# A reversed bias table by 128 one-row transfers on GpSimd's queue, one modulation unit as a block, and key copies on VectorE

## The chip, the cores and the metric

The kernel runs on one core of one Trainium2 chip. The metric is the device time of one execution in microseconds; the kernel before takes 2218.84 us (median of three runs, 2218.35 to 2221.72). It holds two transformer blocks of two layers each, in one program. Each engine (TensorE, VectorE, ScalarE, GpSimd, and SyncE for transfers) runs its own list of instructions in the order in which they are written, and semaphores join the lists.

## The reference

Sequence length 256, width 1024, batch 1, all in float32. The change lies in the two layers of the first block. A layer projects the normed input by one wide matrix into the inputs of three attention branches and their gates:

```
mod = c_act @ w_ada[l] + b_ada[l]
shift, scale, gate = [m[:, None, :] for m in split_cols(mod, (D, D, D))]
h = rms_norm(x, g_pre[l]) * (1.0 + scale) + shift
(cq, ckv, kr, za, qb_, kb_, vb_, zb, qc, kc, vc, zc, gcols) = split_cols(h @ w_in[l], IN_SPLITS)
...
kv = (rms_norm(c_kv, g_kv) @ w_ukv).reshape(B, S, MLA_HEADS, MLA_NOPE + MLA_V)
k_pe = rope(k_r, cos[None], sin[None])
k = jnp.concatenate([kv[..., :MLA_NOPE],
                     jnp.broadcast_to(k_pe[:, :, None, :], (B, S, MLA_HEADS, MLA_ROPE))], axis=-1)
```

Branch a has 8 heads and no bias. Branches b (8 heads, a window of 128, a sink) and c (4 differential heads) add a bias to the scores that depends only on the distance of key and query, `rel_bias[t5_bucket(kpos - qpos)]`, for 12 heads in all. The second block (a recurrent and a forgetting attention mixer, a gated linear attention, a dense and a mixture-of-experts feed-forward) is not touched.

## The kernel before

Activations lie transposed, 128 features by 256 tokens a tile. Weights stream from HBM through `ring`, six slots of 1 MB, filled by SyncE's queue in a fixed order (`stream`). Item n goes into slot n mod 6, and its transfer waits until item n-6 is released (`freed_at`). As the queue is in order, one item that waits holds all behind it.

A projection (`project`) of 128 output columns is 24 matmuls of 128x256: each weight is split into an upper part (`form_upper`, ScalarE, L1465) and a rest (`lower`, VectorE, L2107), and the three products of parts run on lines L697 to L699. ScalarE forms the upper part four projections ahead. The results take four PSUM banks in turn (`claim`): a bank is used again when the instruction that empties it has reported.

**The modulation.** The rows of `w_ada` are weighted and summed on VectorE, a unit (l, i) of two ring items in eight steps (`modulation_step`, L2021 and L2023), after which both slots are released. TensorE then sums over partitions (`modulation`, L887). Unit (0, 4) occupies items 16 and 17. Its eight steps stand two by two between the `lower` calls for the projection `zb`. Item 22, the second half of unit (0, 5), goes into the slot of item 16, and item 23, the weights of `qc`, into the slot of item 17. Item 21 goes into the slot of item 15 (`ukv`), which is released when the projection of the values `va` (L945) is done. Item 27 (`kc`) goes into a slot of unit (0, 5).

**The bias table.** A line of 512 biases per head is computed once (`bias_lines`) and written to HBM (`scratch`, L1605). One transfer on ScalarE's queue (L1614) reads it back into `table_up` with partition p shifted by p, so that the order of the partitions is the wrong way round. TensorE turns it with `flip`, a reversed identity: 12 matmuls of 128x384 (L952), each copied to `table` by ScalarE (L1645). VectorE reads `table` when it adds the bias to the scores of the first head of branch b (L2122).

**The keys of branch a.** The matmuls `kn` give two heads a bank; ScalarE copies each half to its place (`two_heads`), and later copies the rotated rows to all heads (`krows`, L1637 and L1638).

After `ukv` TensorE's order is kn 0 to 3, va 0 and 1, the 12 table matmuls (layer 0 only), kb, vbt, zb 0 to 3, the sum of unit (0, 4), qc 0 to 3, the sum of unit (0, 5), kc 0 to 3, and so on, and then the units of attention (`run_units`), 8 for a branch.

Of the kernel before, what the change touches and what calls it, by code (L numbers as in the profile page):

```python
# [43 lines left out]
def shape_constants(S):  # L44
# [27 lines left out]
    for c in range(4):  # L72
# [3 lines left out]
    flip = np.eye(P)[::-1]  # L76
# [3 lines left out]
               flip=flip, iota=iota)  # L80
# [20 lines left out]
def two_blocks(nc, A, C, out, known):  # L101
# [26 lines left out]
    def sem(name):  # L128
        return ctx.enter_context(nc.semaphore(name))
# [76 lines left out]
    table_up, lines = split(flat[:, 0:12 * 384], 12, 384), flat[:, 4608:5120]  # L206
# [19 lines left out]
    flip = vc[:, 1, 0:P]  # L226
# [123 lines left out]
    ada_ready, modsum_ready, table_ready = sem("ada_ready"), sem("modsum_ready"), sem("table_ready")  # L350
    proj_ready, kb_cleared = sem("proj_ready"), sem("kb_cleared")
    kc_moved, kc_halves = sem("kc_moved"), sem("kc_halves")
# [259 lines left out]
    def _(pe):  # L612
# [190 lines left out]
        def scores(u):  # L803
            br, l, i, _ = u
            b = claim("attn", ("s", br, l, i), *((exp_ready, "exp", br, l, i) if br == "a" else (scored, br, l, i)))
            if br == "a":
                pe.wait_ge(rope_ready, when(rope_ready, "q", l, i))
                pe.wait_ge(proj_ready, when(proj_ready, "krows", l))
# [82 lines left out]
        for l in range(L):  # L891
# [48 lines left out]
            for m_ in range(4):  # L940
                chunk(("kn", l, m_), "gemm", proj_ready, ("kn", l, m_), 1,
                      lambda k: w[:, 0, P * m_:P * m_ + P], lambda k: cq[:, 2])
# [5 lines left out]
            if l == 0:  # L948
                pe.wait_ge(table_in, when(table_in, "all"))
                for i in range(12):  # L950
                    b = claim("gemm", ("table", i), table_ready, "table", i)
                    nc.tensor.matmul(b[:, 0:384], flip, table_up[:, i], start=True, stop=True)\  # L952
                        .then_inc(psum_ready, wrote("table", i))
# [453 lines left out]
    def _(act):  # L1407
# [145 lines left out]
        for l in range(L):  # L1553
# [10 lines left out]
            if l == 0:  # L1564
# [13 lines left out]
                fetch(loaded_tables, flip, C["flip"])  # L1578
# [32 lines left out]
            if l == 0:  # L1611
                act.wait_ge(lines_out, when(lines_out, "all"))
                shifted = bass.AP(tensor=scratch.tensor, offset=0, ap=[[1, P], [512, 12], [1, 384]])
                act.dma_start(table_up, shifted).then_inc(table_in, tick(table_in, "all", by=16))  # L1614
# [16 lines left out]
            for c in range(4):  # L1631
                two_heads("kn", c, k_full)
            for t in range(NT):
                copy_out(("va", l, t), va[:, t], n=512)
            act.wait_ge(rope_ready, when(rope_ready, "k", l))
            every = krope[HEAD:HEAD + ROPE].unsqueeze(1).broadcast_to([ROPE, 4, S])
            nc.scalar.activation(kn[HEAD:HEAD + ROPE], every, ACT.Copy)  # L1637
            nc.scalar.activation(gates[HEAD:HEAD + ROPE, 20:24], every, ACT.Copy)\  # L1638
                .then_inc(proj_ready, tick(proj_ready, "krows", l))
            for n in range(2):  # L1640
                form_behind(("qb1", l), n)
            if l == 0:
# [1292 lines left out]
```

## Time and profile before

| | |
|---|---|
| median of three runs | 2218.84 us (2218.35 to 2221.72) |
| profiled execution | 2218.4 us, of which its span is 2216.6 us |
| TensorE busy (matmul) | 2137.2 us, 96% |
| VectorE busy | 1621.7 us, 73% |
| ScalarE busy | 1292.6 us, 58% |
| GpSimd busy | 26.7 us, 1% |
| granted TensorE clock | 0.979 of full speed, mean |

Matmuls are pipelined and their ends are modelled, so the busy time of TensorE says only that it has work. The places where it has none are read from the timeline and from the chain of waits.

### The profile page before, as it was taken

What the parts mean: (1) busy time and instruction counts of PE and PEld (TensorE: products, weight loads), DVE (VectorE), ACT (ScalarE), POOL (GpSimd) and SP (SyncE); (2) the same over time, 40 slices, a digit from 0 to 9 for tenths busy, and PEclk for the clock granted to TensorE, in tenths of its full rate; (3) what the DMA queues carried; (4) which work ended last, traced back from release to release, by engine and by line L of the source; (5) the groups of instructions that cost most, each with busy time, mean ns of one, the idle gap of its engine ahead of it and who ended that gap; (6) DMA issues with size and microseconds to landing.
All of it is one profiled execution on the core that took longest, in us unless ns stands there. A gap on an engine that the chain in (4) does not pass through costs nothing.

```text
span 2216.6 us, 33306 instructions
## 1 busy us (share of the span) xinstructions
PE 2137.2 (96%) x12812; PEld 1900.1 (86%) x12812; DVE 1621.7 (73%) x1938; ACT 1292.6 (58%) x1560; POOL 26.7 (1%) x19
## 2 busy tenths in 40 slices
PE   6899999999999999999998999999999999999997
PEld 5799999899999989998996888878888888888886
DVE  6557865558855765555636889888888889889896
ACT  2535533555523754433625777777777777777775
POOL 0000000000000300000000000000000000000000
PEclk7999999999999999998999999999999999999999
DMA  9776455556335424553546999989999999999990
GB/s 292 186 225 193 149 156 133 121 189 190 115 115 161 160 84 145 191 172 116 193 147 243 359 349 352 375 319 372 329 360 349 360 335 358 367 331 364 330 365 29
DMA packets 361195, 536.39 MB, mean 242 GB/s; under 512 B 67724, under 2 KB 207936, under 8 KB 361096
## 3 DMA queue, kind: packets, MB, share of 16 engines
q1 hardware_dynamic: 355536, 530.81, 70.1%
q10 hardware_dynamic: 5560, 4.19, 0.6%
q8 instruction: 70, 1.15, 0.2%
q14 instruction: 29, 0.24, 0.0%
HBM read 533.89 MB, written 1.07 MB: 241 GB/s over the span
## 4 chain that ended last, share of the span: by engine, by line
PE 88%; DVE 5%; ACT 3%; issue 2%; DMA 1%; ACTq 0%; DVEq 0%; SPq 0%
PE bank L697 24%; PE bank L699 23%; PE bank L698 23%; PE bank L644 5%; PE bank L849 2%; PE bank L1304 1%; ACT w_hi L1951 1%; PE bank L1252 1%; PE bank L657 1%; PE bank L1351 1%; DVE w_lo L2753 1%; PE bank L832 1%; DVE piece_lo L2385 1%; PE bank L818 1%; PE bank L822 1%
## 5 line engine op out<-in xcount | busy, mean ns | idle before, releaser
L2753 DVE TENSOR_TENSOR w_lo<-pool,w_hi 128x2048 fp32r<-128x2048 f32 x336 | 764.1, 2291 | 110.5 <-ACT w_hi L1951 110.0
L1951 ACT ACTIVATE w_hi<-pool 128x2048 fp32r<-128x2048 f32 x336 | 643.2, 1917 | 140.8 <-PE bank L699 140.8
L697 PE MATMUL bank<-w_hi,xe_hi 128*128 128x512 f32 x896 | 357.9, 399 | 12.7 <-DVE w_lo L2753 8.9
L699 PE MATMUL bank<-w_hi,xe_lo 128*128 128x512 f32 x896 | 350.2, 391 | 0.0
L698 PE MATMUL bank<-w_lo,xe_hi 128*128 128x512 f32 x896 | 349.8, 390 | 0.0
L697 PE MATMUL bank<-h_upper,upper 128*128 128x256 f32 x992 | 295.4, 298 | 3.4 <-DVE h_lo L2197 3.2
L698 PE MATMUL bank<-h_lo,upper 128*128 128x256 f32 x992 | 283.1, 285 | 0.0
L699 PE MATMUL bank<-h_upper,ring_lo 128*128 128x256 f32 x992 | 282.9, 285 | 0.0
L2107 DVE TENSOR_TENSOR ring_lo<-ring,upper 128x1024 fp32r<-128x1024 f32 x132 | 160.4, 1221 | 114.0 <-ACT upper L1465 113.7
L2385 DVE TENSOR_TENSOR piece_lo<-ring,piece_hi 128x1024 fp32r<-128x1024 f32 x118 | 144.9, 1236 | 109.3 <-ACT piece_hi L1454 109.1
L697 PEld LDWEIGHTS bank<-w_hi,xe_hi 128*128 128x128 f32 x896 | 168.6, 188 | 57.2 <-DVE w_lo L2753 17.2
L699 PEld LDWEIGHTS bank<-w_hi,xe_lo 128*128 128x128 f32 x896 | 168.4, 188 | 36.5
L697 PEld LDWEIGHTS bank<-h_upper,upper 128*128 128x128 f32 x992 | 192.6, 194 | 6.5 <-issue 4.5
L698 PEld LDWEIGHTS bank<-w_lo,xe_hi 128*128 128x128 f32 x896 | 168.9, 188 | 33.0
L697 PE MATMUL bank<-left_hi,piece_hi 128*128 128x256 f32 x672 | 193.0, 287 | 2.4 <-DVE left_lo L2407 2.4
L698 PEld LDWEIGHTS bank<-h_lo,upper 128*128 128x128 f32 x992 | 192.7, 194 | 2.0 <-issue 0.5
L699 PEld LDWEIGHTS bank<-h_upper,ring_lo 128*128 128x128 f32 x992 | 192.4, 194 | 0.0
L698 PE MATMUL bank<-left_lo,piece_hi 128*128 128x256 f32 x672 | 190.7, 284 | 0.0
L699 PE MATMUL bank<-left_hi,piece_lo 128*128 128x256 f32 x672 | 190.7, 284 | 0.0
L697 PE MATMUL bank<-w_hi,hT_hi 128*128 128x512 f32 x448 | 175.9, 393 | 0.0
L699 PE MATMUL bank<-w_hi,hT_lo 128*128 128x512 f32 x448 | 174.5, 389 | 0.0
L698 PE MATMUL bank<-w_lo,hT_hi 128*128 128x512 f32 x448 | 174.4, 389 | 0.0
(403 smaller groups left out, 3445.8 us busy)
## 6 DMA issues: line engine op xcount, KB each, us to landing
pool<-in_od_exp_w SPq DMA_DIRECT2D x336, 1024.0 KB, 6.8
ring<-in_w_in SPq DMA_DIRECT2D x48, 1024.0 KB, 5.4
ring<-in_ev_ffn_w SPq DMA_DIRECT2D x33, 1024.0 KB, 5.1
ring<-in_w_ada SPq DMA_DIRECT2D x24, 1024.0 KB, 8.3
ring<-in_od_w_in SPq DMA_DIRECT2D x12, 1024.0 KB, 5.2
ring<-in_ev_w_in SPq DMA_DIRECT2D x10, 1024.0 KB, 5.4
ring<-in_w_in SPq DMA_DIRECT2D x32, 256.0 KB, 4.5
ring<-in_w_out SPq DMA_DIRECT2D x8, 1024.0 KB, 4.8
```

Source lines behind the costliest of these rows:

```text
L644: m = nc.tensor.matmul(b[base:base + rows, 0:cols], left(k), right(k), start=(k == 0), stop=(k == K - 1))
L657: m = nc.tensor.matmul(b[:, at + t:at + t + 1], tile[:, k, P * t:P * t + P], mean[scale][:, 0:1], start=start and t == 0, stop=stop, skip_ ...
L697: nc.tensor.matmul(b, left[0], right[0], start=first, stop=False, skip_group_check=True)
L698: nc.tensor.matmul(b, left[0], right[1], start=False, stop=False, skip_group_check=True)
L699: return nc.tensor.matmul(b, left[1], right[0], start=False, stop=last, skip_group_check=True)
L818: m = nc.tensor.matmul(s, q_full(i)[0:HEAD + ROPE, tok], k_full(i)[0:HEAD + ROPE], start=True, stop=True)
L822: m = nc.tensor.matmul(s, qc[:, i // 2, tok], (kc, kc_odd)[i % 2][:, i // 2], start=True, stop=True)
L849: m = nc.tensor.matmul(b[:, 0:S], v[:, k, at:at + P], pT[:, k], start=(k == 0), stop=(k == NT - 1))
L1951: nc.scalar.activation(w_hi[q % 3], ring_slot(q), ACT.Copy)\
L2107: V.tensor_tensor(dst, src, split(upper[:, n % PIECES], KD, P).bitcast(F32), ALU.subtract)\
L2385: V.tensor_tensor(lo, src, hi.bitcast(F32), ALU.subtract).then_inc(piece_ready, tick(piece_ready, n))
L2753: V.tensor_tensor(w_lo[q % 3], ring_slot(q), w_hi[q % 3].bitcast(F32), ALU.subtract).then_inc(item_vector, tick(item_vector, "lo", q))
```

## The change

The part of the table that turns it on TensorE, with `flip`, `table_up` and the 12 copies on ScalarE, goes. GpSimd issues 128 transfers, one for a partition, which put the shifted line of partition 127-p straight into row p of `table`. VectorE waits for all of them where it first reads the table. Unit (0, 4) becomes one block ahead of the rotation of the keys. The eight key copies of a layer go from ScalarE to VectorE, behind the rotation of the queries, and `krows` goes behind the values of branch c.

```
-            if l == 0:
-                pe.wait_ge(table_in, when(table_in, "all"))
-                for i in range(12):
-                    b = claim("gemm", ("table", i), table_ready, "table", i)
-                    nc.tensor.matmul(b[:, 0:384], flip, table_up[:, i], start=True, stop=True)\
-                        .then_inc(psum_ready, wrote("table", i))
...
-                fetch(loaded_tables, flip, C["flip"])
...
             if l == 0:
                 act.wait_ge(lines_out, when(lines_out, "all"))
-                shifted = bass.AP(tensor=scratch.tensor, offset=0, ap=[[1, P], [512, 12], [1, 384]])
-                act.dma_start(table_up, shifted).then_inc(table_in, tick(table_in, "all", by=16))
...
-            for c in range(4):
-                two_heads("kn", c, k_full)
...
-            if l == 0:
-                for i in range(12):
-                    b = psum(act, "table", i)
-                    nc.scalar.activation(table[:, i], b[:, 0:384], ACT.Copy)\
-                        .then_inc(table_ready, tick(table_ready, "table", i))
...
+            act.wait_ge(rope_ready, when(rope_ready, "k", l))
+            every = krope[HEAD:HEAD + ROPE].unsqueeze(1).broadcast_to([ROPE, 4, S])
+            nc.scalar.activation(kn[HEAD:HEAD + ROPE], every, ACT.Copy)
+            nc.scalar.activation(gates[HEAD:HEAD + ROPE, 20:24], every, ACT.Copy)\
+                .then_inc(proj_ready, tick(proj_ready, "krows", l))
...
             if br != "a":
+                if l == 0:
+                    dve.wait_ge(table_in, when(table_in, "all"))
...
+            if l == 0:
+                modulation(0, 4)
...
+            for c in range(4):
+                b = psum(dve, "kn", l, c)
+                V.tensor_copy(k_full(2 * c)[0:HEAD], b[0:HEAD, 0:S])
+                V.tensor_copy(k_full(2 * c + 1)[0:HEAD], b[HEAD:P, 0:S]).then_inc(kn_ready, tick(kn_ready, l, c))
...
             for c in range(4):
-                two_steps(0, 4, c)
                 lower((("zb" + "1" * (c // 2), l), c % 2))
...
+        pool_engine.wait_ge(lines_out, when(lines_out, "all"))
+        for p in range(P):
+            row = bass.AP(tensor=scratch.tensor, offset=P - 1 - p, ap=[[12 * 512, 1], [512, 12], [1, 384]])
+            pool_engine.dma_start(table[p:p + 1], row).then_inc(table_in, tick(table_in, "all", by=16))
```

On TensorE, this is the place behind the keys and values of branch a (L945 or L944 is va, the rows from L697 or L695 are kb). Before:

```order
L644 MATMUL bank<-pool,ring 128x256 [waits rope_ready] x2
L945 MATMUL bank<-ring,pool 128x512 [waits proj_ready] x2
L952 MATMUL bank<-pool 128x384 [waits proj_ready,table_in]
L952 MATMUL bank<-pool 128x384 [waits proj_ready] x3
L952 MATMUL bank<-pool 128x384 [waits table_ready] x8
L697 MATMUL bank<-h_upper,upper 128x256 [waits lower_ready,table_ready]
L698 MATMUL bank<-h_lo,upper 128x256
```

And now:

```order
L642 MATMUL bank<-pool,ring 128x256 [waits rope_ready] x2
L944 MATMUL bank<-ring,pool 128x512 [waits kn_ready] x2
L695 MATMUL bank<-h_upper,upper 128x256 [waits lower_ready,kn_ready]
L696 MATMUL bank<-h_lo,upper 128x256
L697 MATMUL bank<-h_upper,ring_lo 128x256
```

The 12 matmuls are gone, kb follows va at once, and va waits for the key copies on VectorE.

On VectorE, this is the place where the normed latents are finished (L2269 or L2254) and the rotation of the keys begins (L2275 or L2262). Before:

```order
L2072 RECIPROCAL rstd<-rstd 128x256 [waits root_ready]
L2269 SCALAR_TENSOR_TENSOR pool<-pool,vecs,rstd 128x256 [waits rstd_ready]
L2275 TENSOR_TENSOR tmp<-bank,pool 128x256 [waits psum_ready]
L2276 TENSOR_TENSOR pool<-pool 128x256
L2277 TENSOR_TENSOR pool<-pool,tmp 128x256 [waits dve_step]
```

And now:

```order
L2055 RECIPROCAL rstd<-rstd 128x256 [waits root_ready]
L2254 SCALAR_TENSOR_TENSOR pool<-pool,vecs,rstd 128x256 [waits rstd_ready]
L2004 TENSOR_SCALAR probsT<-ring,small 128x512 [waits slot_loaded5,slot_loaded4,psum_ready]
L2006 SCALAR_TENSOR_TENSOR probsT<-ring,small,probsT 128x512 [waits ada_step] x7
L2262 TENSOR_TENSOR tmp<-bank,pool 128x256 [waits psum_ready]
L2263 TENSOR_TENSOR pool<-pool 128x256
L2264 TENSOR_TENSOR pool<-pool,tmp 128x256 [waits dve_step]
```

The whole of unit (0, 4) stands ahead of the rotation.

On VectorE again, this is the end of the rotation of the queries (L2290 or L2277) and what follows it, down to the memsets behind `zb`. Before:

```order
L2290 TENSOR_TENSOR pool<-pool,tmp 32x256 x3
L2107 TENSOR_TENSOR ring_lo<-ring,upper 128x8x128 [waits upper_ready,rope_ready]
L2021 TENSOR_SCALAR probsT<-ring,small 128x512 [waits slot_loaded5,slot_loaded4,psum_ready]
L2023 SCALAR_TENSOR_TENSOR probsT<-ring,small,probsT 128x512 [waits ada_step]
L2107 TENSOR_TENSOR ring_lo<-ring,upper 128x8x128 [waits upper_ready]
L2023 SCALAR_TENSOR_TENSOR probsT<-ring,small,probsT 128x512 [waits ada_step] x2
```

And now:

```order
L2277 TENSOR_TENSOR pool<-pool,tmp 32x256 x3
L2282 COPY pool<-bank 64x256 [waits psum_ready,rope_ready]
L2283 COPY pool<-bank 64x256
L2282 COPY pool<-bank 64x256 [waits psum_ready]
L2283 COPY pool<-bank 64x256
L2282 COPY pool<-bank 64x256 [waits psum_ready]
L2283 COPY pool<-bank 64x256
L2282 COPY pool<-bank 64x256 [waits psum_ready]
L2283 COPY pool<-bank 64x256
L2090 TENSOR_TENSOR ring_lo<-ring,upper 128x8x128 [waits upper_ready] x5
```

Eight copies have come ahead of the `lower` calls, and the steps of the unit are gone from between them.

## Rows read from the trace of the kernel before

**Rows 1.** The page: the span, and the chain that ended last.

```profile
span 2216.6 us, 33306 instructions
...
PE 88%; DVE 5%; ACT 3%; issue 2%; DMA 1%; ACTq 0%; DVEq 0%; SPq 0%
```

**Rows 2.** Windows: stretch, PE, PEld, DVE, ACT, POOL busy, granted clock, DMA share, GB/s.

```profile
98.00:101.00 3.00, 3.00 (x5) 1.35 (x4) 0.85 (x2) 1.58 (x4) 0.00 (x0) 0.50 0.00 0
...
110.00:128.00 18.00, 17.98 (x148) 17.62 (x146) 4.60 (x7) 6.19 (x10) 0.00 (x0) 1.00 0.53 170
128.00:132.00 4.00, 0.61 (x5) 0.61 (x5) 3.37 (x5) 3.80 (x8) 0.00 (x0) 0.98 1.10 348
132.00:138.00 6.00, 6.00 (x29) 6.00 (x30) 5.93 (x9) 1.06 (x3) 0.00 (x0) 0.50 0.42 133
```

**Rows 3.** Timeline of TensorE: start, length, work, idle before and its releaser.

```profile
97.04 2.93 PE L945 MATMUL bank<-ring,pool 128*128 128x512 f32 x4
99.76 3.43 PE L952 MATMUL bank<-pool 128*128 128x384 f32 x8
105.08 5.43 PE L952 MATMUL bank<-pool 128*128 128x384 f32 x16 [1.89 <-ACT pool L1645]
110.05 0.58 PE L697 MATMUL bank<-h_upper,upper 128*128 128x256 f32 x1
...
131.39 1.46 PE L887 MATMUL bank<-ones,probsT 128*128 128x1 f32 x8 [3.41 <-DVE pool L2096]
```

**Rows 4.** Timeline of SyncE's queue: start and length of the issues.

```profile
71.69 0.37 SPq L2868 DMA_DIRECT2D ring<-in_w_ada  x1
...
100.00 18.37 SPq L2868 DMA_DIRECT2D ring<-in_w_ada  x2
118.41 1.76 SPq L2868 DMA_DIRECT2D ring<-in_w_in  x2
...
139.77 7.71 SPq L2868 DMA_DIRECT2D ring<-in_w_in  x4
```

**Rows 5.** Timeline of ScalarE, where it waited for weights.

```profile
127.50 1.06 ACT L1465 ACTIVATE upper<-ring 128x1024 fp32r<-128x1024 f32 x1 [7.95 <-DMA ring<-in_w_in]
...
145.02 1.06 ACT L1465 ACTIVATE upper<-ring 128x1024 fp32r<-128x1024 f32 x1 [6.36 <-DMA ring<-in_w_in]
```

**Rows 6.** Timeline of VectorE around the two rotations.

```profile
79.21 0.48 DVE L2269 SCALAR_TENSOR_TENSOR pool<-pool,vecs,rstd 128x256 f32<-128x256 f32 x1
84.94 0.42 DVE L2275 TENSOR_TENSOR tmp<-bank,pool 128x256 f32<-128x256 f32 x1 [5.24 <-PE bank L644]
...
94.68 1.76 DVE L2290 TENSOR_TENSOR pool<-pool,tmp 32x256 f32<-32x256 f32 x4
```

**Rows 7.** Groups of VectorE, 62 to 224 us: busy time, mean ns of one.

```profile
L2023 DVE SCALAR_TENSOR_TENSOR probsT<-ring,small,probsT 128x512 f32<-128x512 f32 x21 | 15.7, 749 | 0.4
```

**Rows 8.** Issues on ScalarE's queue: ns min/median/max, and starts.

```profile
L1605 ACTq DMA_DIRECT2D scratch<-pool x1: 357/357/357, 59.8 to 59.8; - x1
...
L1409 ACTq DMA_DIRECT2D pool<-in_g_q x1: 254/254/254, 4.5 to 4.5; - x1
```

**Rows 9.** Transfers: KB each, us from issue to landing.

```profile
ring<-in_w_ada SPq DMA_DIRECT2D x24, 1024.0 KB, 8.3
...
ident<-const_ident SPq DMA_DIRECT2D x1, 64.0 KB, 2.0
```

**Rows 10.** Timeline of VectorE, TensorE and GpSimd where branch b begins.

```profile
226.22 0.75 DVE L2122 SCALAR_TENSOR_TENSOR sbias<-bank,pool 128x256 f32<-128x256 f32 x2
229.92 0.62 DVE L2148 TENSOR_SCALAR sq<-sq,small 128x256 f32<-128x256 f32 x2
...
232.81 0.63 PE L832 MATMUL bank<-ident,sq 128*128 128x128 f32 x4
...
234.38 1.03 POOL L2810 COPY pool<-pool 64x1024 f32<-64x1024 f32 x1 [233.95 <-PE bank L849]
```

**Rows 11.** Timeline of TensorE in layer 1, the last key matmul.

```profile
436.97 1.22 PE L644 MATMUL bank<-pool,ring 128*128 128x256 f32 x2 [1.89 <-DVE pool L2290]
```

More of the change, by code:

```diff
@@ L75, in shape_constants @@
     before = (j < i)
-    flip = np.eye(P)[::-1]
     iota = np.tile(np.arange(P)[None, :], (P, 1))
@@ L79, in shape_constants @@
                chunkmask=chunkmask, restart=restart, pick=pick, before=before,
-               flip=flip, iota=iota)
+               iota=iota)
     return {name: np.ascontiguousarray(a.astype(np.float32)) for name, a in out.items()}
@@ L204, in two_blocks @@
     gates = split(flat, 24, S)
-    table_up, lines = split(flat[:, 0:12 * 384], 12, 384), flat[:, 4608:5120]
+    lines = flat[:, 0:512]
     onehot_sb, window_sb = flat[0:32, 5248:5760], None
@@ L225, in two_blocks @@
     window_sb = vc[0:12, 0]
-    flip = vc[:, 1, 0:P]
     qrope = qc[:, 0:2]
@@ L349, in two_blocks @@
     vecs_ready, mod_ready, const_ready = sem("vecs_ready"), sem("mod_ready"), sem("const_ready")
-    ada_ready, modsum_ready, table_ready = sem("ada_ready"), sem("modsum_ready"), sem("table_ready")
+    ada_ready, modsum_ready = sem("ada_ready"), sem("modsum_ready")
     proj_ready, kb_cleared = sem("proj_ready"), sem("kb_cleared")
-    kc_moved, kc_halves = sem("kc_moved"), sem("kc_halves")
+    kc_moved, kc_halves, kn_ready = sem("kc_moved"), sem("kc_halves"), sem("kn_ready")
     tanh_ready = sem("tanh_ready")
@@ L807, in scores @@
                 pe.wait_ge(rope_ready, when(rope_ready, "q", l, i))
+                pe.wait_ge(kn_ready, when(kn_ready, l, 3))
                 pe.wait_ge(proj_ready, when(proj_ready, "krows", l))
@@ L940, in _ @@
             for m_ in range(4):
-                chunk(("kn", l, m_), "gemm", proj_ready, ("kn", l, m_), 1,
+                chunk(("kn", l, m_), "gemm", kn_ready, (l, m_), 1,
                       lambda k: w[:, 0, P * m_:P * m_ + P], lambda k: cq[:, 2])
@@ L1630, in _ @@
             form_behind(("qb", l), 1)
-            for c in range(4):
-                two_heads("kn", c, k_full)
             for t in range(NT):
                 copy_out(("va", l, t), va[:, t], n=512)
[L1635 to L1639, printed above, removed]
             for n in range(2):
                 form_behind(("qb1", l), n)
-            if l == 0:
-                for i in range(12):
-                    b = psum(act, "table", i)
-                    nc.scalar.activation(table[:, i], b[:, 0:384], ACT.Copy)\
-                        .then_inc(table_ready, tick(table_ready, "table", i))
             b = psum(act, "kb", l, 0)
```

## Prediction

> **What bounds the kernel now.** I read the page first. The span is 2216.6 us, and 88% of the chain that ended last is TensorE [rows 1]. So an edit pays only where TensorE has nothing useful to do, or works at half clock. The windows of layer 0's projections show such places [rows 2]. From 98 to 101 us the granted clock is 0.50 (1.2 GHz). From 128 to 132 us TensorE works 0.61 of 4 us. From 132 to 138 us it is busy but again at 0.50, and one matmul takes 6.00/29 = 0.21 us, where from 110 to 128 us, at 1.00 (2.4 GHz), it takes 18/148 = 0.12 us.
>
> The timeline of TensorE names what lies there [rows 3]. After va, at 97.04, come the table matmuls, with a wait of 1.89 us for ScalarE's copies, and kb starts only at 110.05. At 131.39 stands the sum of unit (0, 4), behind a wait of 3.41 us whose releaser is VectorE's gate of zb. I follow that one back. ScalarE stood for 7.95 us until 127.50, for weights [rows 5]. Those are qc's, issued at 118.41 [rows 4]. They could not be issued earlier, because they go into a slot of unit (0, 4), whose last step ended just then: SyncE's two w_ada issues stretch from 100.00 over 18.37 us, the first at once, the second when the unit let go of its slots. So one late unit on VectorE costs a wait, and then the cold clock behind it.
>
> **The change, part by part.** The sum is made for the profiled execution: 2216.6 us of span and 1.8 us around it, 2218.4 us, which is 0.4 us under the median of 2218.84.
>
> *Table off TensorE.* kb begins where the first table matmul began, at 99.76, rather than at 110.05, plus about 0.3 us that the first matmul of that kind takes to get going in both cases. That is 10.3 us. Against it stand two small costs. The clock is at 0.50 until 101 us at least [rows 2]. Some 6 of kb's matmuls fall into that and cost 0.21 instead of 0.12 us, 0.5 us. And va now waits for the key copies on VectorE. The rotation of the queries ends at 94.68 + 1.76 = 96.44 [rows 6]. The nearest row for a copy out of a bank is the first step of a rotation, 0.42 us for 128x256 [rows 6]; a copy has one operand fewer and half the partitions, so I take 0.35 to 0.42, and the first pair ends at about 97.25, where va started at 97.04: 0.2 us. Later pairs end before TensorE asks for their banks, since one va takes some 1.5 us [rows 3]. Together **-9.6 us** at the end of zb.
>
> In layer 1 the same copies cost nothing. There the last key matmul alone takes 1.22 us [rows 11], longer than a pair of copies (0.8), and va starts behind it. Should that cover be gone it is 0.8 us.
>
> *Unit (0, 4) as a block.* Eight steps of 0.749 us [rows 7] are 6.0 us. VectorE is free from 79.21 + 0.48 = 79.7 until 84.94, 5.24 us of idle time [rows 6]. The second item of the unit was issued at 71.69 [rows 4]. With the median of 8.3 us for such a load [rows 9] it is there at 80.0 at the latest, and the transfer of the table, which shared the queues then, is gone. The block ends at about 85.8 to 86.1. The rotation of the keys is some 1 us late, and nobody waits for it within that: kn and the queries' rotation come later. So the slots are free at 86 instead of 118. Item 21 still goes at 100.0, when va is done, and items 22 and 23 (qc) follow within 1 us instead of 18. Three loads of 1 MB at the 348 GB/s of [rows 2] need 9.0 us and some 2 to start, so qc's weights land at about 111. TensorE ended zb at 131.39 - 3.41 = 128.0 and now does so at 118.4, and finds everything ready: qc's weights have their upper part and rest 2.3 us after they land, at 113.3. The wait of 3.41 us goes. With it goes the cold clock, from 131.4 to 138 us. The sum itself takes 1.46 us there, and I take 0.5 off it, and 2.6 off the 29 matmuls that follow (29 x 0.09). **-6.5 us.**
>
> *What is late next.* kc's weights wait for unit (0, 5). They were issued at 139.77 and there at 145.02, 5.25 us [rows 4, 5]. Its steps stand between the gates of zb and the `lower` calls of qc. Paced by TensorE, which is some 10 us early, and with its tiles there at 109, VectorE ends them at about 124, 16 us earlier. The load lands at 129.2, ScalarE and VectorE need 2.3 us, and TensorE could start kc at 131.1. **+0.4 us.** After that all shifts alike.
>
> *ScalarE.* It loses 12 table copies and 8 key copies a layer, and `krows` moves by 2 us of work to a place where TensorE has more than 10 us of projections ahead of the first scores. The uppers of zb are formed earlier. Zero on the path.
>
> The sum is -9.6 - 6.5 + 0.4 = **-15.7 us, about 2203 us**, if the table is there in time.
>
> **The 128 transfers.** This is the unknown. GpSimd issues none before, so no row gives a price. The line is written at 59.8 + 0.36 us [rows 8] and needs some 2 us to land [rows 9], so GpSimd starts at about 62.3. Branch b adds its first bias at 226.22 [rows 10], which becomes 210.5. VectorE waits there for all 128. With 2 us for the last to land, the queue has 146 us, **1.14 us a transfer**. The bounds: a small transfer on ScalarE's hardware queue is issued in 0.254 us [rows 8], 128 in 33 us. If each held the queue until it has landed, 2.0 us as the small `ident` load takes [rows 9], it would be 256 us. I take 1.0 us, nearer to the middle than to either end, since the queue need not wait for a landing, but GpSimd makes the list of pieces (12 for a transfer) itself. Then the queue ends at about 190 and the wait costs nothing. That is a choice, and the least certain number here.
>
> The Trainium skill, DMA: Bandwidth & Descriptors, "Anatomy of one DMA", gives a fixed cost of some 2.0 us a transfer from GpSimd, and says that most of it is the receipt after the last byte and little the making of the descriptors. By the first half alone the sum would be an estimated 256 us and the table 110 us late; by the second, the transfers overlap and the table is in time. No row here shows GpSimd's part.
>
> **The rivals.** *The table is late* (the other side). VectorE stands at branch b's first bias, and behind that wait lie all its later work: the rests of the gate weights, the probabilities, the outputs, and so TensorE. From the bias at 226.22 to the probabilities' scaling at 229.92 and their turning on TensorE at 232.81 [rows 10] there are some 2.3 us of slack (232.81 less 229.92 + 0.62). Each further microsecond costs one, and a long wait costs another 3 in clock, as above. At 1.25 us a transfer the gain is used up. At 1.4 us the queue ends at 241.5 + 2, 33 us late, and the time is 2203 + 31 + 3 = 2237. At 2.0 us it is 2203 + 110 = 2313. For it speaks that the price is unknown between 0.25 and 2.0, against it that it must be in the upper part. GpSimd's key move at 234.38 [rows 10] is queued behind too, but is needed only by branch c. Chance 0.24 (slower), and 0.07 each for a little late (5 to 11 us of gain left) and for a wash.
>
> VectorE's own work could press on the same price, if its instructions of one input held up GpSimd. Up to 210 us these are the scalings of branch a's eight heads, 0.62 us a head [rows 10], and little else. If each of them stopped the queue, that is 5 us, and the limit would fall from 1.14 to 1.10 us. The Trainium skill, SBUF — State Buffer, the box on the "DVE blocks DMA" trap, states such a lock: GpSimd can't write descriptors while VectorE runs a copy or tensor_scalar in its two-port mode. No row before shows it.
>
> *The unit's block does not free the slots early*, or the loads of qc are slowed by the row transfers beside them: then the wait at 131.39 is partly kept, and 3 to 6 us of the gain with it. The gain would be 9 to 12 us, 2207 to 2210. Against it: 18 KB a microsecond is 18 of some 350 GB/s, and qc's weights are ready 5 us before TensorE asks for them. Chance 0.10.
>
> *No change at all*, because what is saved is waited for later: with 88% of the chain on TensorE [rows 1], little behind this stage waits for a transfer or an engine that would not move with it. It is in the 0.07 of the wash.
>
> **How the numbers follow.** In time, with the whole gain: 0.52. Part of it kept back: 0.10. A little late: 0.07. All faster, 0.69. Within 0.2% (4.4 us, about what a measurement of this kernel tells from none) 0.07, slower 0.24. The likeliest case has its own range, 2200 to 2207. The range for 8 in 10 reaches down to 2199, if the cold clock at 98 us shrinks too, and up to 2240, a price of 1.4 us a transfer.
>
> **What would show it.** kb's matmuls start right behind va near 100 us. The sum of unit (0, 4) has no wait, the granted clock is 1.00 from 102 us on, and its second w_ada issue stands at about 100.4. GpSimd's queue shows 128 issues from 62 us; their spacing decides. Right: no idle time at VectorE's first biased score near 210 us. Wrong: a wait there with the transfers as its releaser, TensorE idle and at 0.50 behind it.

## The result, and the profile after

Timed side by side, the changed kernel takes 2231.02 us (median of 7 runs, 2228.5 to 2239.0) and the kernel before 2220.34 (7 runs, 2218.4 to 2222.6): ratio 1.0049, interval 1.0037 to 1.0061. It is slower by some 11 us, where a gain, to 2203 us, was forecast. The profiled execution took 2232.15 us.

The page of the changed kernel: span and the chain that ended last.

```profile
span 2230.3 us, 33397 instructions
...
PE 86%; DVE 5%; DMA 3%; ACT 3%; issue 2%; ACTq 0%; DVEq 0%; SPq 0%
```

The chain now holds 3% of DMA, where it had 1% [rows 1]. GpSimd's queue, and the statistics of its line (ns min/median/max, starts; then the time from issue to landing):

```profile
62.13 65.48 POOL L2801 DMA_DIRECT2D pool<-scratch  x128 [61.69 <-DMA scratch<-pool]
...
L2801 POOL DMA_DIRECT2D pool<-scratch x128: 518/518/758, 62.1 to 127.1; - x128
...
DMA to landing us min/median/max: 2.3/5.6/16.7
```

The issues are cheap, one each 0.518 us, and end at 127.6. But the last rows land up to 16.7 us after their issue, so something is backed up. TensorE's timeline, to be held against [rows 3]:

```profile
98.04 1.22 PE L642 MATMUL bank<-pool,ring 128*128 128x256 f32 x2 [1.89 <-DVE pool L2277]
99.05 3.07 PE L944 MATMUL bank<-ring,pool 128*128 128x512 f32 x4
101.56 0.68 PE L695 MATMUL bank<-h_upper,upper 128*128 128x256 f32 x1
...
132.00 1.87 PE L886 MATMUL bank<-ones,probsT 128*128 128x1 f32 x8 [12.41 <-DVE pool L2079]
...
147.81 0.58 PE L695 MATMUL bank<-h_upper,upper 128*128 128x256 f32 x1 [5.80 <-DVE pool L2079]
```

kb starts at 101.56 instead of 110.05. TensorE is through with zb at 132.00 - 12.41 = 119.6, before at 128.0: the table's departure did pay, 8.4 us. Then comes a wait of 12.41 us where 3.41 stood. The same two hops as before lead to the cause. SyncE's queue (start and length of the issues) against [rows 4], and ScalarE's two waits against [rows 5]:

```profile
102.15 0.99 SPq L2863 DMA_DIRECT2D ring<-in_w_ada  x2
103.19 5.38 SPq L2863 DMA_DIRECT2D ring<-in_w_in  x2
113.66 12.82 SPq L2863 DMA_DIRECT2D ring<-in_w_ada  x2
```

```profile
128.11 1.06 ACT L1458 ACTIVATE upper<-ring 128x1024 fp32r<-128x1024 f32 x1 [16.95 <-DMA ring<-in_w_in]
...
143.66 1.06 ACT L1458 ACTIVATE upper<-ring 128x1024 fp32r<-128x1024 f32 x1 [12.73 <-DMA ring<-in_w_in]
```

qc's weights are two loads of 1 MB, issued between 103.19 and 108.57, 15 us earlier than before, as forecast. The first arrived at 128.11: 24.9 us for 1 MB, where before it took 9.1 (118.41 to 127.50). The second arrived at 143.66, and behind it stands TensorE's wait of 5.80 us, two projections after the sum. So rather more was lost than the one wait of 12.41 us shows. The windows (stretch, PE, PEld, DVE, ACT, POOL busy, granted clock, DMA share, GB/s) say what the queues did:

```profile
104.00:108.00 4.00, 4.00 (x36) 4.00 (x35) 3.18 (x3) 2.56 (x5) 4.00 (x9) 1.00 1.09 337
...
116.00:120.00 4.00, 3.59 (x30) 3.38 (x29) 0.00 (x0) 0.00 (x0) 4.00 (x9) 1.00 1.16 91
120.00:124.00 4.00, 0.00 (x0) 0.00 (x0) 0.00 (x0) 0.00 (x0) 4.00 (x8) 0.73 1.17 121
...
132.00:136.00 4.00, 4.00 (x18) 4.00 (x19) 2.82 (x4) 0.00 (x0) 0.00 (x0) 0.50 1.21 90
136.00:140.00 4.00, 4.00 (x24) 4.00 (x24) 0.00 (x0) 0.00 (x0) 0.00 (x0) 0.63 1.17 85
...
152.00:156.00 4.00, 4.00 (x34) 4.00 (x33) 0.00 (x0) 0.25 (x1) 0.00 (x0) 0.93 1.03 344
```

The last two columns belong together. (The share adds up the queues' packets on the 16 transfer engines, so it can pass 1.) In the four slow windows the engines are busy all the time (share 1.16 to 1.21), and move 85 to 121 GB/s, a quarter to a third of the 348 of [rows 2]. So they are held up while they carry a packet. The slow stretch lasts beyond the last issue of a row at 127 us. And behind the wait of 12.41 us the granted clock is at 0.50, as behind the shorter one before.

### The profile page after: what moved, and what is told of

It reads as the page before. It is cut to its first block, busy times and chain, and to the rows that moved or that the text cites. A ratio compares the mean times of both kernels' runs of the same rounds, so it can differ in the third digit from the quotient of the medians.

```text
span 2230.3 us, 33397 instructions
## 1 busy us (share of the span) xinstructions
PE 2132.1 (96%) x12788; PEld 1897.4 (85%) x12788; DVE 1629.6 (73%) x1954; ACT 1280.7 (57%) x1532; POOL 92.1 (4%) x147
## 3 DMA queue, kind: packets, MB, share of 16 engines
q0 software_dynamic: 4096, 2.37, 0.9%
## 4 chain that ended last, share of the span: by engine, by line
PE 86%; DVE 5%; DMA 3%; ACT 3%; issue 2%; ACTq 0%; DVEq 0%; SPq 0%
PE bank L695 23%; PE bank L697 23%; PE bank L696 23%; PE bank L642 5%; DMA ring<-in_w_in 2%; PE bank L848 1%; PE bank L1297 1%; ACT w_hi L1934 1%; PE bank L1245 1%; PE bank L655 1%; PE bank L1344 1%; DMA ring<-in_w_ada 1%; DVE w_lo L2743 1%; DVE probsT L2006 1%; PE bank L831 1%
## 5 line engine op out<-in xcount | busy, mean ns | idle before, releaser
L695 PE MATMUL bank<-w_hi,xe_hi 128*128 128x512 f32 x896 | 358.0, 400 | 12.8 <-DVE w_lo L2743 8.9
L697 PE MATMUL bank<-w_hi,xe_lo 128*128 128x512 f32 x896 | 350.4, 391 | 0.0
L695 PE MATMUL bank<-h_upper,upper 128*128 128x256 f32 x992 | 297.4, 300 | 11.1 <-DVE pool L2079 5.8
L697 PE MATMUL bank<-h_upper,ring_lo 128*128 128x256 f32 x992 | 284.6, 287 | 0.0
L695 PEld LDWEIGHTS bank<-w_hi,xe_hi 128*128 128x128 f32 x896 | 168.7, 188 | 57.1 <-DVE w_lo L2743 17.3
L695 PEld LDWEIGHTS bank<-h_upper,upper 128*128 128x128 f32 x992 | 194.4, 196 | 14.7 <-issue 6.9
L697 PEld LDWEIGHTS bank<-w_hi,xe_lo 128*128 128x128 f32 x896 | 168.5, 188 | 36.2
L695 PE MATMUL bank<-left_hi,piece_hi 128*128 128x256 f32 x672 | 192.7, 287 | 2.8 <-DVE left_lo L2397 2.8
L697 PEld LDWEIGHTS bank<-h_upper,ring_lo 128*128 128x128 f32 x992 | 194.1, 196 | 0.0
L697 PE MATMUL bank<-left_hi,piece_lo 128*128 128x256 f32 x672 | 190.2, 283 | 0.0
L695 PE MATMUL bank<-w_hi,hT_hi 128*128 128x512 f32 x448 | 176.1, 393 | 0.0
L697 PE MATMUL bank<-w_hi,hT_lo 128*128 128x512 f32 x448 | 174.6, 390 | 0.0
```

Of the source, the lines that this page charges most:

```text
L695: nc.tensor.matmul(b, left[0], right[0], start=first, stop=False, skip_group_check=True)
L697: return nc.tensor.matmul(b, left[1], right[0], start=False, stop=last, skip_group_check=True)
```

## The experiments

Executions begin a little differently: ScalarE's issue of the write of the lines, before which all these kernels are alike, lies between 58.5 and 62.3 us. So I read positions from that mark. The table has the time from the mark to the start of TensorE's sum of unit (0, 4), with its wait, and to GpSimd's key move in layer 0 [rows 10], a place behind all that the change touches there. These two columns are from one profiled execution of each kernel. Only medians and ratios give the times. The kernels were timed in several sets, each beside the kernel before, whose median lay between 2219.2 and 2222.2 us; medians of two sets can differ by that much for no cause in the kernel, and the ratios allow for it. "Un-rev." marks the kernels whose table isn't reversed; the rest of their work is the same.

```
                                     median   ratio (interval)          to the sum [wait]  to the move
before                                                                     71.6 [3.4]        174.6
changed                              2231.0   1.0049 (1.0037-1.0061)       72.2 [12.4]       185.5
e1  one transfer, ScalarE, un-rev.   2206.9   0.9942 (0.9925-0.9959)       59.2 [0]          159.1
e5  one transfer, GpSimd, un-rev.    2204.6   0.9928 (0.9912-0.9943)       58.6 [0]          158.3
e11 e1, key copies on ScalarE        2206.9   0.9926 (0.9907-0.9945)       59.1 [0]          158.9
e8  e1, unit in steps                2212.0   0.9969 (0.9956-0.9982)       63.9 [5.2]        165.7
e4  changed, unit in steps           2227.1   1.0029 (1.0018-1.0039)       68.1 [9.9]        178.0
e2  rows from 138 us                 2262.1   1.0184 (1.0167-1.0201)       58.6 [0]          214.7
e3  rows on SyncE's queue            2258.0   one run                      95.3 [26.1]       210.8
e6  12 pieces to 12 partitions       2207.6   0.9948 (0.9933-0.9963)       58.6 [0]          162.3
e12 12 pieces from one line          2231.4   1.0044 (1.0029-1.0060)       73.1 [13.4]       186.5
e14 12 pieces to 2 partitions        2219.9   0.9993 (0.9984-1.0003)       63.8 [4.1]        172.3
e9  row order 37 n                   2215.9   0.9977 (0.9968-0.9987)       61.6 [3.4]        170.2
e16 row order by the map             2215.1   0.9975 (0.9966-0.9985)       62.6 [3.9]        169.8
e17 row order against the map        2241.4   1.0089 (1.0062-1.0116)       92.8 [3.1]        194.6
e7  16 copies, 8 transfers           2213.4   0.9968 (0.9955-0.9980)       68.0 [0]          168.0
e10 the same at 160 us               2210.1   0.9950 (0.9936-0.9964)       58.0 [0]          162.2
e13 the same at 85 us                2211.5   0.9960 (0.9946-0.9973)       62.0 [3.4]        163.9
e15 the same, one at a time          2206.5   0.9932 (0.9918-0.9946)       58.6 [0]          161.2
```

In e17 three more waits of TensorE, 23 us in all, lie ahead of the sum, and in e7 one of 8.3 us.

My theory (A) was that the row transfers slow the loads beside them; the rival (B) that the unit's block, which sends more loads off together, does it.

**e1, one transfer instead of 128.**

```
+                shifted = bass.AP(tensor=scratch.tensor, offset=0, ap=[[1, P], [512, 12], [1, 384]])
+                act.dma_start(table, shifted).then_inc(table_in, tick(table_in, "all", by=16))
```

> The 128 row transfers are left out; in their place the one transfer of before (all 128 partitions, 2304 KB, ScalarE's queue) fills the table, so that its rows are not reversed and the output differs in branches b and c. Unit (0, 4) as a block and the key copies on VectorE stay. Theory A (the row transfers beside the weight loads slow these down): the bandwidth from 80 to 145 us is back at about 350 GB/s, qc's weights land by about 112 us, TensorE doesn't wait for 12.4 us at the sum of unit (0, 4), and the time is 2201 to 2207 us, 24 to 30 under the changed kernel. Theory B (the unit's block and its three or four loads in a row are what slows qc's weights): the wait at the sum of the unit stays and the time is 2220 or more.

2206.9 us: A, B falls. The same 2.36 MB from the same lines into the same tile leave no wait at the sum here; as rows they cost 24.2 us more. The granted clock is 1.00 (2.4 GHz) from 107 to 168 us.

**e4 and e8, the unit in steps, with rows and without.** The block goes, `two_steps(0, 4, c)` comes back ahead of each `lower` of zb; e8 has e1's transfer as well.

> The changed kernel with unit (0, 4) back in two steps ahead of each lower of zb, the rows as they are. Theory A: the rows slow the loads all the same; the slots of the unit come free later still, qc's weights are issued later, and the time is 2231 to 2240. Theory B: the loads are apart again, as before, the wait for qc goes back to about 3 us, and the time is 2208 to 2215.

> One transfer into the table on ScalarE's queue (not reversed, so the output differs in branches b and c), and unit (0, 4) back in two steps ahead of each lower of zb. This takes apart the two terms of the forecast: by it the unit's block is worth 6.5 us, so that this kernel should be at 2206.9 + 6.5 = 2213 us (2211 to 2216) with a wait of 3 to 11 us at the sum of unit (0, 4), since TensorE is some 10 us earlier than before and the slots still come free at about 118 us. If the block was worth nothing, 2206 to 2209.

Without rows, the block is worth 165.7 - 159.1 = 6.6 us to the key move and 5.1 in the medians, near the forecast (6.5). With rows it costs 3.9 us in the medians. e4 (2227.1) lies outside both of its cases: I expected it to be no faster than the changed kernel, and it is. So the rows cost 15.1 us beside the unit in steps (e4 less e8) and 24.2 beside the block (changed less e1): the rest of the 24 comes only from the two together. In e4 qc's first weights left at 109.66 and needed 13.1 us, in the changed kernel they left at 103.19 and needed 24.9. What exactly makes the earlier set of loads fare worse beside the rows was not taken apart.

**e11, key copies back on ScalarE.**

> One transfer into the table on ScalarE's queue (not reversed, so the output differs in branches b and c), unit (0, 4) as a block, and the key copies back on ScalarE ahead of the copies of va, as before, in both layers. The forecast priced their move to VectorE at +0.2 us or nothing: 2204 to 2209, no difference from the 2206.9 of the same kernel with the copies on VectorE. If the move to VectorE is what held back va, 2202 to 2204; if ScalarE is the tighter engine there, 2210 or more.

2206.92 against 2206.86: no effect of the move of the copies can be seen.

**e2, the rows later.** One more wait ahead of the first row:

```
+        pool_engine.wait_ge(psum_ready, when(psum_ready, "kc", 0, 0))
```

> The same 128 row transfers on GpSimd's queue, but their first one waits until TensorE has ended kc's first head (about 133 us if nothing is late before). Theory A: no wait at unit (0, 4), TensorE some 15 us ahead at 133 us. At 0.518 us each the rows are issued until about 200 us and need, with loads beside them, 5 to 20 us more, so that branch b's first bias at about 210 us waits 0 to 10 us, and loads from 140 to 200 us are slowed; 2203 to 2215 us. Theory B: it stays at 2228 or more, since the block of the unit and its loads are as in the changed kernel.

The first half came as expected, no wait at the unit. The second was far off: 2262.1. The windows of this kernel while its rows are under way:

```profile
160.00:180.00 20.00, 17.42 (x137) 16.67 (x136) 5.60 (x7) 5.64 (x8) 20.00 (x40) 1.00 1.18 119
180.00:220.00 40.00, 0.00 (x0) 0.00 (x0) 0.00 (x0) 0.00 (x0) 23.22 (x46) 0.51 1.13 87
```

TensorE stands for 53 us, because gate weights came in at a trickle: three loads of 1 MB needed a median of 57.7 us. B is out here too, since the unit was long done. Moving the rows moves the damage.

**e3, the rows on SyncE's queue**, 13 behind each of ten loads.

> The same 128 rows on SyncE's hardware queue, 13 of them behind each of the ten weight loads from 66 us on, so that rows and weights share one queue. If the software queue of GpSimd as such is what slows the weights, the rows cost only their bytes (2.36 MB, some 7 us at 350 GB/s) and the issue time on SyncE, and the time is 2205 to 2215. If the shape is what costs (12 pieces of 1536 bytes from one place of memory into one partition), the bandwidth stays under 200 GB/s from 70 to 140 us here as well, and the time is 2225 or more.

2258.0 us, but not for the reason that I gave, so this run doesn't decide its question. A row takes 0.688 us to issue on SyncE; the 128 held up the weight loads behind them by some 90 us. Between loads the DMA share was 0.1 to 0.2 and the loads themselves landed in a median of 6.7 and 7.6 us: at this pace, 26.8 GB/s with no loads beside them, the rows show no backlog.

**e5, e6 and e12, queue or shape.** e5 is e1's transfer on GpSimd's queue. e6 and e12 keep 12 pieces of 1536 bytes a transfer and GpSimd's pace:

```
e6   piece = bass.AP(tensor=scratch.tensor, offset=512 * i + rows.start, ap=[[10, 12], [1, 384]])
     pool_engine.dma_start(table[g:g + 111:10, i], piece)
e12  row = bass.AP(tensor=scratch.tensor, offset=512 * (p % 12) + p % 10, ap=[[12 * 512, 1], [10, 12], [1, 384]])
     pool_engine.dma_start(table[p:p + 1], row)
```

> The 128 row transfers are left out; one transfer of the same 1536 pieces of 1536 bytes into all 128 partitions fills the table, as in the run with one transfer, but issued by GpSimd, on its software queue, at about 62 us. The table's rows are not reversed, so the output differs in branches b and c. Theory S (the software queue itself holds up the weight loads beside it): bandwidth falls under 250 GB/s while it runs, it needs 25 us or more rather than 12.8, and the time is 2212 or more. Theory D (the shape of the transfers: 12 pieces at a time into one partition): it lands in 12 to 16 us, its packets take about 68 ns each as on ScalarE's queue, and the time is 2203 to 2209.

> 132 transfers on GpSimd's queue with the same pieces of 1536 bytes, at most 12 a transfer, from 62 us on, but the 12 pieces of one transfer go to 12 partitions that lie 10 apart rather than to one. The table's rows are not reversed, so the output differs in branches b and c. Theory D (one partition at a time takes the bytes of all engines, and weights queue behind): the packets take about 70 ns, weight loads beside them stay near 350 GB/s, no wait over 2 us at the sum of unit (0, 4), 2203 to 2210 us. If instead many small transfers as such are what costs (their number, their end marks, the software queue), it stays at 2222 or more with packets of 1024 bytes at 80 ns or more.

> 128 transfers on GpSimd's queue, each of 12 pieces of 1536 bytes into one partition, as in the changed kernel, but the 12 pieces are read from one line, 10 elements apart, as in the run with spread rows. The table's content is another, so the output differs in branches b and c. It is the control for that run, where both the target and the source were other than in the changed kernel. If the target (one partition) is the cause: 2225 to 2236, packets of 1536 bytes at 110 ns or more. If the source was (12 places 2048 bytes apart): 2203 to 2212.

e5 clears the software queue, e6 the number of transfers and their end marks, e12 the source. What is left is the target: 12 pieces into 12 partitions 2207.6 us, into one 2231.4. (Even e6 reaches the key move 4 us behind e5, with a wait of 3.2 us for kc.) The queues from 62 to 145 us (packets, MB, share of 16 engines), of the changed kernel:

```profile
q1 hardware_dynamic: 18277, 11.05, 79.5%
q0 software_dynamic: 4096, 2.37, 24.2%
```

of e6:

```profile
q1 hardware_dynamic: 24195, 16.32, 70.1%
q0 software_dynamic: 4224, 2.37, 13.5%
```

and of e1, where q10 is the one transfer:

```profile
q1 hardware_dynamic: 24819, 16.38, 69.8%
q10 hardware_dynamic: 1576, 2.38, 8.1%
```

The same bytes hold the engines three times as long as rows (24.2% to 8.1%), and the weights beside them are hit harder: 11.05 MB in 79.5% of 83 us is 167 GB/s, in e1 16.38 MB in 69.8% is 283.

**e14, e9, e16 and e17, what in the target.** e14 sends a transfer to two partitions, 64 apart (un-reversed). The others only change the order of the changed kernel's rows, for n from 0 to 127:

```
e9   p = 37 * n % P
e16  p = 64 * (n // 8 % 2) + 32 * (n // 64) + 4 * (n % 8) + n // 16 % 4      # 0, 4, 8, ... 28, 64, ...
e17  p = 64 * (n // 64) + 32 * (n % 2) + 4 * (n // 8 % 8) + n // 2 % 4       # 0, 32, 1, 33, 2, 34, ...
```

> 128 transfers on GpSimd's queue, each of 12 pieces of 1536 bytes, but 6 of them into one partition and 6 into another, 64 apart (not reversed, so the output differs in branches b and c). The transfers under way together still go to neighbours. If the number of pieces that meet in one partition sets the cost, it falls by about half of the 24 us between 2231 and 2207: 2215 to 2222, packets of 1536 bytes between 100 and 155 ns. If anything short of a wide spread chokes in the same way: 2226 or more.

> The changed kernel, its 128 rows issued in another order (row 37 n modulo 128 as the n-th), so that rows under way together lie far apart; the table is the same. If what chokes is something that neighbouring partitions share, rows on the way no longer press on the same place: packets of 1536 bytes near 80 ns, no wait over 3 us at the sum of unit (0, 4), 2203 to 2212 us. If it is the 12 pieces of one transfer meeting in one partition, the order changes nothing: 2227 to 2235.

> The changed kernel with its 128 rows in the order 0, 4, 8, ... 28, 64, 68, ... 92, 1, 5 and so on. The Trainium skill, SBUF — State Buffer, section Door 1 (the DMA port swizzle), says that memory's DMA side has 16 ports of 8 partitions each, 4 neighbours and the 4 that lie 32 further; by that, this order gives each of 16 rows in a row a port of its own. If a port is what chokes: at least as good as the order by 37 (2215.9 us), 2206 to 2215 us, waits at unit (0, 4) under 4 us, no backlog. If only the distance of neighbouring rows counts, it is no better: 2216 to 2222, since rows under way together are here but 4 apart.

> The changed kernel with its rows in the order 0, 32, 1, 33, 2, 34, 3, 35, 4, 36 and so on: neighbours are never issued one behind the other, but by the map of that section each eight in a row share one port. If a port chokes: as slow as the changed kernel or slower, 2228 to 2240, with a backlog of rows at the end. If neighbouring partitions as such are the cause: faster than the changed kernel, near the order by 37, 2214 to 2222.

e14 came in the expected middle, 2219.9. (Its bytes travelled in other packets, 6144 where the changed kernel has 4096, most of the bytes in larger ones. So more than the number of partitions was changed, that part of the expectation can't be read, and the middle place has no single cause.) e9, 2215.9, lies between its two cases: far order takes away most of the cost, not all. The order alone moves the time from 2215.1 to 2241.4 us. The windows from 80 to 145 us, for e16 and e17:

```profile
80.00:145.00 65.00, 53.42 (x349) 48.90 (x348) 38.53 (x66) 24.61 (x43) 47.84 (x94) 0.90 1.06 225
```

```profile
80.00:145.00 65.00, 37.86 (x197) 31.47 (x196) 24.22 (x45) 14.21 (x25) 49.49 (x98) 0.78 1.17 122
```

e16 sends rows only 4 apart and is as good as the wide scatter, but its 2215.1 lies on the bound between its two cases, so e17 decides. e17 never sends neighbours one behind the other; by distance alone it should have been faster than the changed kernel, and it is the slowest. So it isn't distance but the group. These are the groups that the Trainium skill, SBUF — State Buffer, section Door 1, gives as the 8 partitions of one port, and both runs agree with its map. The Trainium skill, DMA: Bandwidth & Descriptors, Back-pressure in remote DMA, says that a saturated target port clogs the way back to the engines and to what shares it. It says so for transfers between cores; the high share at low bandwidth here agrees with it for loads from memory.

How much one group takes is less sure. A row is 18,432 bytes, and one every 0.518 us is 35.6 GB/s. All 2.36 MB were in by 143 us, 81 us after the start, in e2 from 137.7 to 224, 86 us: 29 and 27 GB/s on average. The Trainium skill, DMA: Bandwidth & Descriptors, Where 436 GB/s comes from, gives 435 GB/s for 16 ports, from which I get an estimated 27.2 for one; the two averages are of that size. But they are averages. GpSimd's queue (packets, MB, share of 16 engines) in the changed kernel from 70 to 100 us, and from 100 to 140:

```profile
q0 software_dynamic: 1953, 1.13, 26.4%
q0 software_dynamic: 1821, 1.07, 26.9%
```

and in e17 from 70 to 100 us, and from 100 to 130:

```profile
q0 software_dynamic: 1523, 0.80, 36.9%
q0 software_dynamic: 1951, 1.15, 43.6%
```

That is 37.7 and 26.8 GB/s in the one, 26.7 and 38.3 in the other, with weights going to the same groups beside them. In e17 the rows kept up for 30 us although eight in a row share a group; at a median of 10.8 us from issue to landing some 20 rows are under way, so more than one group can be filling. The rate of a single group was therefore not measured. What is shown is that rows back up in stretches, and that the order over the groups decides how far.

**e7, e10, e13 and e15, the reversed table by few transfers.** The lines are written 16 times, so that a transfer with a positive step takes 16 rows 8 apart:

```
-    scratch = nc.dram_tensor("scratch", (12, 512), F32, kind="Internal").ap()
+    scratch = nc.dram_tensor("scratch", (16, 12, 512), F32, kind="Internal").ap()
...
+                act.dma_start(scratch.rearrange("c r n -> r c n"), lines[0:12, :].unsqueeze(1).broadcast_to([12, 16, 512]))\
...
+        for g in range(8):
+            rows = bass.AP(tensor=scratch.tensor, offset=P - 1 - g,
+                           ap=[[12 * 512 - 8, 16], [512, 12], [1, 384]])
+            pool_engine.dma_start(table[g:g + 121:8], rows).then_inc(table_in, tick(table_in, "all", by=16))
```

e10 waits for zc's first head ahead of them, e13 for unit (0, 4), e15 ahead of each for another event:

```
+        for g, ended in enumerate((("zb", 3), ("qc", 1), ("qc", 3), ("kc", 1), ("kc", 3), ("vc", 0), ("vc", 1), ("zc", 0))):
+            pool_engine.wait_ge(psum_ready, when(psum_ready, ended[0], 0, ended[1]))
```

> The same reversed table with 8 transfers instead of 128. The lines are written 16 times into memory (393 KB rather than 24), one behind the other, so that a transfer can take 16 rows that lie 8 apart with a positive step (each row from the next copy): 192 pieces into 16 partitions a transfer, on GpSimd's queue. If the rows' shape or number is what costs: the table lands within 15 to 20 us, nothing waits at unit (0, 4), and the time is 2203 to 2210, that is a ratio of 0.993 to 0.997 to the kernel before. ScalarE's wait for the write of the lines may grow by 1 to 3 us, near TensorE's first waits at 80 us. If the software queue itself is at fault: over 2212.

> The kernel with sixteen copies of the lines and eight transfers, whose first transfer now waits until TensorE has ended zc's first head (about 160 us). The second w_ada item of unit (0, 4) no longer shares the queues with the table, so VectorE's wait of 8.9 us for it and TensorE's of 8.3 us at the first query matmul go. The table is due at about 210 us and should land by 185. Expected 2203 to 2208 us, 5 to 8 under the kernel with the same eight transfers at 67 us. If the write of the sixteen copies (7 us) is what made the weights late, 3 us or more of the wait stay and it is over 2208.

> Sixteen copies of the lines, eight transfers, the first of them held back until VectorE has ended unit (0, 4), about 87 us. Then neither that unit's second item (which the transfers delayed at 67 us) nor the gate weights near 170 us (which they delayed at 160 us) share the queues with the table, but kvb's and zb's weights, issued at 80 to 95 us, do. If those have slack, no wait over 2 us in TensorE from 100 to 220 us and 2204 to 2208 us. If not, kb or zb starts late: a wait of 3 us or more near 100 to 110 us and 2209 or more.

> Sixteen copies of the lines and eight transfers of 288 KB again, but one at a time: each waits for another event of TensorE between the end of zb and zc's first head (about 118 to 160 us, some 6 us apart). The three moments tried so far each put all eight beside loads that were needed soon, and each cost TensorE 3 to 8 us. If only the bunching costs, no wait over 1.5 us stands in TensorE from 100 to 220 us and the time is 2204 to 2208 us, as with one transfer. If any transfer beside these loads costs, 2209 to 2212 as with the others.

All four beat both kernels. e7 made VectorE wait 8.9 us for the unit's second item, and TensorE 8.3 us behind it: the block stands ahead of the rotation of the keys, so its weights have become urgent. e10 (2210.1) was expected at 2208 at most; it kept a wait of 2.8 us at TensorE where the eight ran beside gate weights. e13 (2211.5) was expected under 2208; zb's pieces were late, and with them the issue of qc's weights and the sum (3.4 us). One at a time, from 121 to 162 us, none of these waits is left, and 2206.45 us lies among the un-reversed kernels' times (2204.6 to 2206.9): 0.68% under the kernel before, interval 0.54 to 0.82%. TensorE's waits in it from 95 to 225 us (us in total, times, longest):

```profile
PE bank L642 <- DVE pool L2278: 3.2, 2, 1.9
PE bank L831 <- DVE sq L2134: 1.1, 1, 1.1
PE bank L848 <- ACT probsT L1517: 0.9, 1, 0.9
PE bank L695 <- DVE ring_lo L2091: 0.8, 1, 0.8
```

The first, for the rotation of the queries, stands in all these kernels; the last is kc's.

## Why the prediction was wrong

*Table off TensorE, -9.6 us: right.* In e5 TensorE is through with zb 58.6 us from the mark, before 131.39 - 3.41 - 59.76 = 68.2: 9.6. In the changed kernel it is 59.8, so 8.5: VectorE waited 1.81 us for the unit's second item, and the keys with it. In e1, with one transfer, the same wait is 1.1 us, and in e5 there is none, so the rows account for a part of it at most. The forecast called that item there in time.

*Key copies.* 0.42 and 0.43 us each, at the upper end of the 0.35 to 0.42 taken or just above it; no effect (e11). VectorE at that place in the changed kernel:

```profile
81.58 0.49 DVE L2004 TENSOR_SCALAR probsT<-ring,small 128x512 f32<-128x512 f32 x1 [1.81 <-DMA ring<-in_w_ada]
...
98.02 0.42 DVE L2282 COPY pool<-bank 64x256 f32<-64x256 f32 x1
98.44 0.43 DVE L2283 COPY pool<-bank 64x256 f32<-64x256 f32 x1
```

*Unit (0, 4) as a block, -6.5 us: right without rows* (6.6 to the key move, 5.1 in medians), of the other sign with them. *kc, +0.4:* 0.7 to 0.8 us in e5 and e1. *The sum, -15.7:* e1 and e5 gain 15.5 and 16.3 us to the key move, and 13.7 and 14.6 in the medians. Behind that move executions differ by some 2 us either way, so no cause can be given for the rest.

*The 128 transfers, nothing if in time: the step that failed.* Issue was priced at 1.0 us between 0.25 and 2.0; it is 0.518, and the table was in time. VectorE has no wait at its first biased score:

```profile
236.78 0.76 DVE L2107 SCALAR_TENSOR_TENSOR sbias<-bank,pool 128x256 f32<-128x256 f32 x2
```

Nowhere does VectorE's work visibly hold up GpSimd's issue, which takes 0.518 us at the median and 0.758 at most: the lock that the Trainium skill, SBUF — State Buffer, "DVE blocks DMA", states did not appear. That is a weak test: of copies and scalings of wide tiles, VectorE ran only one scaling (0.49 us) and the eight key copies out of banks (3.4 us) from 62 to 128 us. The fixed 2.0 us of the Trainium skill, DMA: Bandwidth & Descriptors, "Anatomy of one DMA", agrees with the shortest landing, 2.3 us, and lay beside the next issues, as its second half says. But the forecast looked only at what the transfers wait for, not at what waits for them. The mechanism was there as a rival, "the loads of qc are slowed by the row transfers beside them", at 0.10 and 3 to 6 us, and was waved away with "18 KB a microsecond is 18 of some 350 GB/s". This is the faulty sentence, and with it the term of 0 us for the transfers. It divides by the rate of all sixteen groups, as if it didn't matter where a row goes. The runs show that it does: the same pieces by about as many small transfers on the same queue take no longer than one wide transfer (2206.9) when each is spread over 12 partitions (e6, 2207.6), and the order of the rows alone moves the time by 26 us (e16, e17). The term measured 24.2 us in the medians (e1 against the changed kernel), more than the whole gain of 13.7. By the estimate of 27 GB/s for one group, a row a microsecond would have been 18 of 27, and a row every 0.518 us is 35.6, over it: the cheaper issue, a good sign in the forecast, would then be what makes the backlog. No run sent the rows more slowly beside the loads, so this is not shown. Open too is why the block of the unit, worth 5.1 us by itself, costs 3.9 beside the rows.

The rival on the other side, a late table, was wrong too, though its sign came out. The measured time lies inside the range, which was stretched upwards for a late table. That is luck, not the range's reasoning.

## What to carry to other kernels

Price a transfer by where it lands, too: ask how many groups of partitions it reaches (the estimate of 27 GB/s for one group was of the right size here), and whether its neighbours in the queue go to the same ones. Where a profile shows a high DMA share at a low rate, look for a narrow target among the transfers under way; its own latency looks harmless (5.6 us here), and the victims are the wide loads beside it. If rows must be brought one by one, order them round the groups; better, let each transfer reach 16 partitions, and send them singly into gaps between the loads.

## What had not been expected of the hardware

The order of 128 equal transfers changes this kernel by 26 us (2215.1 to 2241.4). A one-row transfer of 12 pieces is issued faster by GpSimd (0.518 us) than by SyncE's hardware queue (0.688). The write of the 16 copies, 384 KB out of 12 partitions, took from 60.7 to 67.1 us in e7, and ukv's two loads beside it a median of 5.9 us, against 3.7 in e5; whether the few partitions or the 384 KB do it was not tested. Even the best order of rows stays 8 us behind one transfer (2215.1 to 2206.9); whether that is the 12 pieces that meet in one partition was not tested apart.
